# Two-layer hybrid trunk on one core: split weight parts kept in DRAM for a layer's second half, and a planner that counts DMA and PSUM banks

## The reference

```python
h = rmsnorm(x, pre_norm)
proj = jnp.einsum('bld,de->ble', h, w_in)          # 1024 -> 26 x 256 columns and 24 small ones
o_a = rmsnorm(gated_deltanet(silu(conv(gq, gk, gv)), gb, ga), gdn_norm) * silu(gz)      # 4 heads of 128
o_b = rmsnorm((ssd(silu(conv(sx, sB, sC)), sdt) + D * x) * silu(sz), ssd_norm)          # 16 heads of 64, 2 groups
o_c = rmsnorm(retention(rotary(rq), rotary(rk), rv), ret_norm) * silu(rg)               # 4 heads of 128
out = jnp.einsum('ble,ed->bld', concatenate([o_a, o_b, o_c]), w_out)
x = x + rmsnorm(out, post_norm)
```

## Time and profile before

| | before |
|---|---|
| median of 3 runs | 2435.17 us (2432.48 to 2436.13) |
| the profiled execution | 2434.56 us, its span 2432.8 us |
| TensorE busy | 2317.5 us, 95% |
| VectorE / ScalarE / GpSimd busy | 1385.3 / 884.9 / 913.6 us |
| mean granted TensorE clock | 0.993 |
| moved by DMA | 175.68 MB |

### The profile page before, as it was taken

One profiled execution on the slowest core, in us unless ns is written; L12 is line 12 of the kernel. 1 busy time (PEld: TensorE's weight loads), 2 busy tenths in 40 slices (PEclk: granted clock), 3 DMA queues, 4 the chain that ended last, 5 costly groups with the idle time before them and its releaser, 6 DMA issues.

```text
span 2432.8 us, 37233 instructions
## 1 busy us (share of the span) xinstructions
PE 2317.5 (95%) x15032; PEld 2060.2 (85%) x15032; DVE 1385.3 (57%) x2268; ACT 884.9 (36%) x1599; POOL 913.6 (38%) x752
## 2 busy tenths in 40 slices
PE   5999989999999999999999999999999999999995
PEld 4787878999887888899888788889988878889995
DVE  3766577435666658734566656763455664773333
ACT  3644334223534434323353434412343442442200
POOL 2554433233544343333254433323334443342310
PEclk9999999999999999999999999999999999999998
DMA  3211111223211112322221111322321111131212
GB/s 129 76 53 52 53 35 45 78 87 104 70 61 44 61 45 96 104 70 88 103 70 61 44 53 47 119 87 74 106 81 61 60 45 53 61 113 62 87 53 96
DMA packets 33722, 175.68 MB, mean 72 GB/s; under 512 B 3984, under 2 KB 4752, under 8 KB 20112
## 3 DMA queue, kind: packets, MB, share of 16 engines
q1 hardware_dynamic: 32832, 171.85, 20.8%
q10 hardware_dynamic: 720, 1.45, 0.2%
HBM read 164.90 MB, written 8.39 MB: 71 GB/s over the span
## 4 chain that ended last, share of the span: by engine, by line
PE 72%; DVE 5%; issue 3%; DMA 1%; ACT 0%; POOL 0%; SPq 0%; DVEq 0%; ACTq 0%; POOLq 0%
PE ps L955 68%; PE ps L958 5%; DVE wk L1410 1%; DMA xfin<-x_mid 1%; DMA w_loaded<-in_w_in 0%; DVE wk L1387 0%; DVE gss L1363 0%; DVE slot L1316 0%; DVE gss L1372 0%; ACT junk L1709 0%; DVE acc L1503 0%; DVE wk L1390 0%; DVE wk L1394 0%; DVE wk L1402 0%; DVE acc L1589 0%
## 5 line engine op out<-in xcount | busy, mean ns | idle before, releaser
L1896 POOL TENSOR_TENSOR w_low<-w_loaded,w_hi 128x512 fp32r<-128x512 f32 x416 | 569.9, 1386 | 719.8 <-ACT w_hi L1644 719.6
L955 PE MATMUL ps<-w_hi,hT_hi 128*128 128x256 f32 x1792 | 530.8, 296 | 1.2 <-POOL w_low L1896 1.2
L955 PE MATMUL ps<-w_low,hT_hi 128*128 128x256 f32 x1792 | 505.7, 282 | 0.0
L955 PE MATMUL ps<-w_hi,hT_lo 128*128 128x256 f32 x1792 | 500.6, 279 | 0.0
L955 PE MATMUL ps<-wo_loaded,mixT 128*128 128x256 f32 x2048 | 459.6, 380 | 12.7 <-DVE wk L1376 12.1
L955 PEld LDWEIGHTS ps<-wo_loaded,mixT 128*128 128x128 f32 x2048 | 383.5, 190 | 68.7 <-DVE wk L1376 14.0
L955 PEld LDWEIGHTS ps<-wk 128*128 128x128 f32 x2336 | 297.2, 191 | 84.3 <-issue 29.7
L955 PE MATMUL ps<-wk 128*128 128x128 f32 (+2 forms) x2336 | 343.6, 286 | 18.6 <-DVE mixT L1489 4.0
L955 PEld LDWEIGHTS ps<-w_low,hT_hi 128*128 128x128 f32 x1792 | 340.9, 190 | 1.2 <-issue 0.2
L955 PEld LDWEIGHTS ps<-w_hi,hT_hi 128*128 128x128 f32 x1792 | 337.8, 189 | 3.6 <-POOL w_low L1896 2.0
L955 PEld LDWEIGHTS ps<-w_hi,hT_lo 128*128 128x128 f32 x1792 | 339.8, 190 | 0.0
(11 more groups left out here) (179 smaller groups left out, 2825.7 us busy)
## 6 DMA issues: line engine op xcount, KB each, us to landing
w_loaded<-in_w_in SPq DMA_DIRECT2D x104, 1024.0 KB, 4.9
wo_loaded<-in_w_out SPq DMA_DIRECT2D x64, 512.0 KB, 3.6
wk<-in_x SPq DMA_DIRECT2D x8, 512.0 KB, 4.2
xfin<-in_x SPq DMA_DIRECT2D x8, 512.0 KB, 5.4
x_mid<-acc SPq DMA_DIRECT2D x8, 512.0 KB, 2.9
wk<-x_mid SPq DMA_DIRECT2D x8, 512.0 KB, 3.6
xfin<-x_mid SPq DMA_DIRECT2D x8, 512.0 KB, 4.3
out<-acc SPq DMA_DIRECT2D x8, 512.0 KB, 2.9
```

The lines of the kernel that those rows point to most:

```text
L955: return nc.tensor.matmul(o, a, b, start=start, stop=stop)
L1896: tt(w_lo[at], wr[at], w_hi[at], ALU.subtract)\
```

## The change

- **Kept parts.** A DRAM scratch `w_split` holds the high and low parts of all 26 pieces. In parts 0 and 2, once a piece's first half is projected, SP stores both parts (entry `keep`, 2 transfers of 1 MB), and the next load of that ring slot waits for them (`w_kept`). In parts 1 and 3 SP loads the two parts instead of the raw piece, and no `split` steps stand in the plan for these pieces. Every load of a piece is now cut in two by columns, with a semaphore for each half (`w_in_sem[slot][j]`): two transfers of 0.5 MB in parts 0 and 2, four in parts 1 and 3. TensorE waits for `w_lo_ready` four times in a piece as before in parts 0 and 2, and for the load twice in parts 1 and 3.
- **The planner counts DMA.** It has a DMA clock: 3200 ns for 1 MB, 1700 more until a transfer has landed, for the loads and kept stores of input pieces (`load_piece`, `MB`).
- **The planner counts banks.** `bank_due` gives the time when the banks that a step needs are emptied; it enters `due` and TensorE's own clock. `emptied_by_act` says which engine empties a bank.
- **Choices.** `NEAR` goes from 150 to 300, `OUT_WAIT` from 1500 to 1000, `LATE` from 99999 to 0, so a slice that isn't due gives way to a step or `out` unit. An `out` unit is only taken if it is itself due within `NEAR`, and a missing `split` no longer counts as stuck.

The core of the diff:

```diff
@@ front_steps
-                    if 0 <= j < 4 and not odd and (p, i) != (PARTS - 1, len(PIECES) - 1):
+                    if 0 <= j < 4 and not odd and (p + (i == len(PIECES) - 1)) % 2 == 0 and (p, i) != (PARTS - 1, len(PIECES) - 1):
@@ make_plan
+    def dma(work, *after):
+        return run("dma", work, *after) + 1700
+    def load_piece(n, after=()):
+        for half in range(2):
+            at["w_in", n, half] = dma(MB if n // len(PIECES) % 2 else MB // 2, *after)
...
-            out = [("w_lo", n, kk // 2)] if half == 0 else []
+            out = [("w_in", n, kk // 4) if p % 2 else ("w_lo", n, kk // 2)] if half == 0 else []
...
-        pe = lambda w: run("pe", w, *after)
+        pe = lambda w: run("pe", w, *after, "banks")
...
-                mark(("w_in", n + W_RING), end + 5000)
+                load_piece(n + W_RING, ("n", ))
+            elif p % 2 == 0:
+                dma(2 * MB, ("w_lo", n, 3))
...
+    def bank_due(step):
+        tags = [tag for pool, tag in bank_uses(step) if pool == "mix"]
+        times = []
+        for j, tag in enumerate(tags):
+            n = len(held) + j - len(MIX_BANKS)
+            if 0 <= n < len(held):
+                times.append(at.get(("emptied", held[n]), FAR) - 440 * j)
+        return max(times, default=0)
...
+        for pool, tag in bank_uses(step):
+            if pool == "mix":
+                held.append(tag)
+                if (step[0], tag[-1]) != ("gdn_turn", "v"):
+                    at["emptied", tag] = clock["act" if emptied_by_act(step, tag) else "dve"] + 60
+        if step[0] == "gdn_x0":
+            at["emptied", ("gdn_turn", *step[1:], "v")] = clock["dve"] + 60
...
-        return max([at.get(e, 0) for e in needs(step)], default=0)
+        return max([at.get(e, 0) for e in needs(step)] + [bank_due(step)])
...
-        if outs and ("small", smalls) in done and (late or stuck or wait > OUT_WAIT and apart >= APART):
+        unit = outs[0] if outs and ("small", smalls) in done else None
+        if unit and due(unit) <= now + NEAR and (late or stuck or wait > OUT_WAIT and apart >= APART):
...
-        elif not front_needs:
+        elif not front_needs and (not late or not (step or unit)):
...
-OUT_WAIT = 1500
-LATE = 99999
-NEAR = 150
+OUT_WAIT = 1000
+LATE = 0
+NEAR = 300
@@ sync
                     if n >= W_RING:
                         wait_filled(sp, ("proj", *divmod(n - W_RING, len(PIECES)), 1))
-                    sp.dma_start(wr[:, n % W_RING, :], w_in[p // 2, key[2]]).then_inc(w_in_sem[n % W_RING], 16)
+                        sp.wait_ge(w_kept[n % W_RING], kept_done(n - W_RING))
+                    for j in range(2):
+                        cols = slice(j * KD * PC // 2, (j + 1) * KD * PC // 2)
+                        if p % 2 == 0:
+                            sp.dma_start(wr[:, n % W_RING, cols], w_in[p // 2, key[2]][:, cols]).then_inc(w_in_sem[n % W_RING][j], 16)
+                        else:
+                            sp.dma_start(w_hi[:, n % W_RING, cols].bitcast(F32), w_split[key[2], 0][:, cols]).then_inc(w_in_sem[n % W_RING][j], 16)
+                            sp.dma_start(w_lo[:, n % W_RING, cols].bitcast(F32), w_split[key[2], 1][:, cols]).then_inc(w_in_sem[n % W_RING][j], 16)
+                elif kind == "keep":
+                    sp.wait_ge(S["w_lo_ready"], 4 * split_no(n) + 4)
+                    sp.dma_start(w_split[key[2], 0], w_hi[:, n % W_RING, :].bitcast(F32)).then_inc(w_kept[n % W_RING], 16)
+                    sp.dma_start(w_split[key[2], 1], w_lo[:, n % W_RING, :].bitcast(F32)).then_inc(w_kept[n % W_RING], 16)
@@ tensor, proj
-                            pe.wait_ge(S["w_lo_ready"], 4 * n + kk // 2 + 1)
+                            if p % 2 == 0:
+                                pe.wait_ge(S["w_lo_ready"], 4 * split_no(n) + kk // 2 + 1)
+                            elif kk % 4 == 0:
+                                pe.wait_ge(w_in_sem[n % W_RING][kk // 4], loads_done(n))
```

More of the change, by code:

```diff
@@ L489, in play @@
             mark(("xf", p, r[0] + 1), clock["dve"] + 5500)
+    for n in range(W_RING):
+        load_piece(n)
     done, smalls = {("small", -1)}, -1
@@ L493, in make_plan @@
     turns = [("mix_turn", p, g) for p in range(PARTS) for g in range(GROUPS)]
+    held = []
+    def bank_due(step):
[6 more added lines that the diff above has]
+        return max(times, default=0)
     def emit(step):
         plan.append(step)
+        at["banks"] = bank_due(step)
         play(step)
         done.add(step)
+        for pool, tag in bank_uses(step):
[5 more added lines that the diff above has]
+            at["emptied", ("gdn_turn", *step[1:], "v")] = clock["dve"] + 60
         if step[0] == "split_small":
@@ L552, in make_plan @@
         late = not front_needs and due(front[front_at][0]) > now + LATE
-        stuck = any(n and n[0] != "rescale" for n in front_needs) or front_at == len(front)
-        if outs and ("small", smalls) in done and (late or stuck or wait > OUT_WAIT and apart >= APART):
+        stuck = any(n and n[0] not in ("split", "rescale") for n in front_needs) or front_at == len(front)
+        unit = outs[0] if outs and ("small", smalls) in done else None
+        if unit and due(unit) <= now + NEAR and (late or stuck or wait > OUT_WAIT and apart >= APART):
             emit(outs.pop(0))
             apart = 0
-        elif not front_needs:
+        elif not front_needs and (not late or not (step or unit)):
             apart += front[front_at][0][0] == "proj"
@@ L560, in make_plan @@
             front_at += 1
-        elif front_needs[0] and front_needs[0][0] in ("split", "rescale"):
+        elif front_needs and front_needs[0] and front_needs[0][0] in ("split", "rescale"):
             chain = sides["split" if front_needs[0][0] == "split" else "scale"]
@@ L564, in make_plan, with emptied_by_act, split_no, loads_done @@
         else:
-            later = [x for x in (step, side, *turns[:1]) if x and known(x)]
+            later = [x for x in (step, side, unit, *turns[:1], *([] if front_needs else [front[front_at][0]])) if x and known(x)]
+            later = [due(x) for x in later if due(x) < FAR]
             assert later, (mix[mix_at:mix_at + 1], front[front_at:front_at + 1], front_needs)
-            clock["pe"] = max(now + 1, min(due(x) for x in later))
+            clock["pe"] = max(now + 1, min(later))
     return plan
+def emptied_by_act(step, tag):
+    k = step[0]
+    return (k in ("small", "small2", "gdn_x0", "x_turn") or k == "gdn_p" and tag == step
+            or (k, tag[-1]) in (("gdn_turn", "q"), ("gdn_s", "q"), ("bc_turn", 0), ("ret_turn", "k")))
 def half_after(p, i, half):
     return ("proj", p, i + half, 1 - half, Q - 1)
-OUT_WAIT = 1500
-LATE = 99999
+OUT_WAIT = 1000
+LATE = 0
 SPLIT_FROM = 6
 APART = 20
-NEAR = 150
-SLICE, LINE, TURN, UNIT, TABLE = 705, 224, 109, 16 * 216, 1283
+NEAR = 300
+FAR = 1e12
+SLICE, LINE, TURN, UNIT, TABLE, MB = 705, 224, 109, 16 * 216, 1283, 3200
+def split_no(n):
+    return n - len(PIECES) * ((n // len(PIECES) + 1) // 2)
+def loads_done(n):
+    return sum(32 if m // len(PIECES) % 2 else 16 for m in range(n % W_RING, n + 1, W_RING))
+def kept_done(n):
+    return sum(32 for m in range(n % W_RING, n + 1, W_RING) if m // len(PIECES) % 2 == 0)
 def slot_of(p, i, half):
@@ L681, in hybrid_kernel @@
     x1 = nc.dram_tensor("x_mid", (SEQ, D), F32, kind="Internal").ap()
+    w_split = nc.dram_tensor("w_split", (len(PIECES), 2, P, KD * PC), F32, kind="Internal").ap()
     with ExitStack() as ctx:
@@ L761, in hybrid_kernel @@
         loaded = sem("consts_loaded")
-        w_in_sem = [sem(f"piece_loaded{i}") for i in range(W_RING)]
+        w_in_sem = [[sem(f"piece_loaded{i}_{j}") for j in range(2)] for i in range(W_RING)]
+        w_kept = [sem(f"piece_kept{i}") for i in range(W_RING)]
         wo_in = [sem(f"unit_loaded{i}") for i in range(2)]
@@ L842, in hybrid_kernel @@
             loads.append((where[release] if n >= W_RING else -2, n, ("in", p, i)))
+            if p % 2 == 0:
+                loads.append((where["proj", p, i, 0, Q - 1], n, ("keep", p, i)))
         for n in range(PARTS * NT):
```

13 lines of the change are left out of this document (8 added, 5 removed).

## The result

| | before | after |
|---|---|---|
| median, us | 2435.44 (5 runs, 2432.48 to 2439.86) | 2444.73 (5 runs, 2443.67 to 2446.74) |
| ratio after / before | | 1.0038, 95% interval 1.0023 to 1.0052 |
| the profiled execution, its span | 2434.56, 2432.8 | 2446.74, 2444.9 |
| TensorE busy | 2317.5 us | 2334.6 us |
| mean granted TensorE clock | 0.993 | 0.992 |

The change makes the kernel 9.3 us slower, 0.38%. The forecast was 2438, and the result lies in the likeliest case's own range of 2425 to 2452; slower had the largest chance, 0.43. The margin between gain and loss was small, and this result lies on the side of the second rival: more direct pairs than forecast, though without its clock falls. The two profiled executions lie 12.1 us apart in span, 2.8 more than the medians, so what is read from the two traces adds up to more than 9.3.

A forecast was written before the change was run, and what follows sets the result against it. TensorE, busy 95% of the span, was taken to bound the kernel. Terms -24 (banks), -1 (low parts), +22 (direct pairs), +4, +2 and 0 gave +3 us: 2435.2 to 2438, likeliest 2425 to 2452, wide 2408 to 2470.

The forecast's parts named there:

- the likeliest case: Whole kernel: bank savings and direct-pair costs nearly cancel, 2438 us, own range 2425 to 2452; chance 0.40.
- the second rival: DeltaNet stages: all pairs become direct, costing 36 us instead of 22, and the clock falls, 14 us: 2466; chance 0.22.
- Part 1, splits: ScalarE and GpSimd splits dropped in the second halves: TensorE does not wait there, 0 us, between 0 and -2.
- Part 2, transfers: Kept stores and larger loads on the SP queue: covered by projection time, 0 us, bounds -1 and +8.
- Part 3, banks: TensorE's waits for full PSUM banks in parts 1 to 3: 24 us of 28.4 saved, bounds 0 and 30.
- Part 4, direct pairs: DeltaNet `gdn_s`/`gdn_v` and `gdn_o`/`gdn_s` without a slice between: 53 pairs at 0.41 us, +22 us, bounds 0 and 45.
- Other steps early: Some 16 other steps come a little early under NEAR 300, 0.25 us each: +4 us, bounds 0 and 12.
- Single `out` units: `out` units put singly between slices by OUT_WAIT and LATE: 20 more changes of 0.09 us, +2 us (0 to 6).
- that the pairs don't come: DeltaNet chunks: VectorE is busier in the model, so banks pay and pairs seldom become direct: 2414 us; chance 0.27.
- the slower one: The second rival, all pairs direct and clock falls: 2466 us, deciding from about 60 direct pairs without any fall; chance 0.22.
- That the transfers bind: Pieces that stand back to back: 0.3 us late for each of some 26, 8 us, 2446; chance 0.05.
- That the plan hardly changes: Planner: modelled bank emptying is too early, so bank waits stay and NEAR acts little: 2435 us; chance 0.06.

The follow-up runs named there:

- e1: Kernel before with the change's DRAM scratch, stores and half loads, its old order of steps, without splits in parts 1 and 3: 2433.74 us, ratio 0.9984.
- e8: Changed kernel without kept parts, every piece loaded raw and split in every part, planner as changed: 2447.16 us, ratio 1.0042.
- e9: Changed kernel with NEAR 150, OUT_WAIT 1500 and LATE 99999 as before, bank and DMA counting and kept parts retained: 2451.78 us, ratio 1.0064.
- e6: Changed kernel with the modelled `resid` and `state` VectorE times 310 instead of 300 ns in parts 1 and 3 alone: 2429.86 us, ratio 0.997.
- e5: Changed kernel with the modelled VectorE copies of `ret_turn` at 1350 instead of 1250 ns: 2439.73 us, ratio 1.0013.
- e10: Changed kernel with `resid` and `state` 310 ns in parts 1 and 3, `ret_turn` 1350, `ret_o` state work 350 instead of 250: 2421.39 us, ratio 0.9941.
- e2: Changed kernel with NEAR alone set back from 300 to 150: 2433.98 us, ratio 0.9986.
- e4: Changed kernel with the modelled state update of `gdn_o` at 310 instead of 300 ns in all parts: 2447.5 us, ratio 1.0041.

## Why the prediction was right, and where its steps were off

The mechanism was right, banks against direct pairs with transfers and splits at nothing, and so was the likelier sign (0.43 against 0.38 for faster). The size of the sum, +3 us, was too small, and that it came so near is in part luck: the banks gave about 13 us more than said and what stood against them took about 24 more. By its steps:

- **Part 1, splits: 0 said, between 0 and -2.** e1 has -3.4 for splits and transfers together, e8 no gain that can be told from none. VectorE did get faster as GpSimd fell silent. Windows of part 1 (busy of PE, PEld, DVE, ACT, POOL, clock, DMA share, GB/s), against the earlier trace rows:

```profile
588.00:1180.00 592.00, 581.37 (x3771) 512.38 (x3769) 314.61 (x567) 168.53 (x290) 90.43 (x87) 1.00 0.35 115
1180.00:1772.00 592.00, 579.82 (x3746) 512.21 (x3745) 345.81 (x566) 217.14 (x404) 230.12 (x183) 1.00 0.48 169
```

  GpSimd falls from 228.1 to 90.4 us, VectorE from 345.2 to 314.6 with the same 567 instructions, and the part takes 3.5 us longer. The Trainium skill (SBUF — State Buffer, Who interferes with whom) says that a VectorE instruction with two SBUF inputs contends with a GpSimd instruction that reads SBUF. The trace agrees: 30.6 us of VectorE time vanish in the part without splits, and the mean of the convolution's operation falls from 1080 to 969 ns. The time shows none of it.

- **Part 2, transfers: 0, right by e1, with a step that was too small.** SP was said to be held 2 to 6 us by a piece's stores (and 0.5 MB in 3.6 us is 146 GB/s, not 142). The stores land after 7.7 and 9.7 us (median), above all rows, and SP's own row of waits is

```profile
SPq L981 <- DMA w_split<-w_low: 374.8, 47, 11.9
```

  that is 8.0 us each and 11.9 at the longest, a little over the upper bound of 11.6. The cover held: TensorE waits for no DMA, and its waits for low parts grow by 2.8 us only. The sum of that part stood on the spacing of the pieces, and not on the price of a store. The share of the queue, 39%, was right. The Trainium skill (DMA: Bandwidth & Descriptors, Bandwidth) asks for transfers of 1 MiB and more. The trace agrees in kind: a raw half of 0.5 MB lands in the 4.9 us that a whole piece took the earlier trace rows. In the time the cut cost nothing that e1 shows.

- **Part 3, banks: -24 said (-25 with the low parts), -38 found.** This is a term mis-sized. All of the 28.4 us of listed waits went, no rest stayed; from start to start they are 31.7 (13.7, 13.5 and 4.5). On top went the 6.7 us behind line 1468 in part 0, listed with 6.5, which the rows showed and the sum left in place. The waits for low parts, from which 1 us was to come, grew instead. In the parts where nothing else interferes e9 shows the net of it, -5.8 and -8.3 us, where the sum has 8 a part. The price of a change from a mixing product to a projection, 0.09 us, was misread. The second product of a slice does come 0.09 late, but the first comes early by nearly as much. In before, eight `wk` products followed by a wide slice:

```profile
654.74 1.05 PE L955 MATMUL ps<-wk 128*128 128x128 f32 x8
655.55 0.48 PE L955 MATMUL ps<-hT_hi,w_hi 128*128 128x512 f32 x1
655.87 0.40 PE L955 MATMUL ps<-hT_hi,w_low 128*128 128x512 f32 x1
```

  Such products follow each other after 0.11 us, so seven steps are 0.78, and the slice starts 0.03 us after the eighth product. Over the 233 such entries into a narrow slice in before the two steps together take 0.232 us (median), where 0.11 and 0.12 back to back are 0.229. A change costs next to nothing. The price of a direct pair stands, for it was counted from 698.25, which is already such an early start.

- **Part 4, direct pairs: +22 said, +27.5 found.** 67 new ones instead of 53: the share of 60% was too low. The two orders aren't alike: `gdn_s` to `gdn_v` is direct in 47 of the 48 places counted, so the other VectorE work that was to push it past the 4 ns of margin hardly stood there; `gdn_o` to `gdn_s` is direct in 27 of 48. The price of 0.41 was good: 0.41 on average by the ledger (0.43 for the first kind, 0.37 for the second), 0.47 by e6.

- **Other steps early: +4 said, about +10 found** in the two kinds that were traced, within 0 to 12. The ledger has 4.6 us more from slices to other `wk` steps; if those are of this kind too, which wasn't tested, it is 14, above the bound. `ret_s` (12 x 0.4 us; e5: -5.0 without it) and `ret_o` (4 x 1.1, 4.9 by the ledger; e10: at most about -2) both fall under NEAR = 300. I hadn't gone through the model's lines for the retention as I had for `gdn_s`: at 300 each mark whose lead is between 150 and 300 changes its step, and they can be listed from the planner's code alone.

- **Single `out` units: +2,** not tested by itself. It was 20 more changes at 0.09 us. The plan enters the projection from other work 491 times and not 537; 67 pairs alone would make it 470, so 21 more did come from elsewhere, but at the price just found they cost nothing that can be told.

The rivals: that the pairs don't come is refuted by the timeline. Of the slower one, half came true: it was to decide from 60 pairs without any fall of the clock, and there were 67. In the DeltaNet stages of parts 1 to 3 the clock never fell in after. The stretch that was slow in before is at full clock; of the slow ones that stand elsewhere, this one in part 0 lies behind a wait of 2.7 us for a low part:

```profile
216.00:220.00 4.00, 3.07 (x23) 2.66 (x23) 1.27 (x4) 0.96 (x3) 0.00 (x0) 1.00 0.96 362
...
239.00:244.00 5.00, 3.59 (x10) 2.90 (x11) 4.93 (x5) 3.22 (x5) 5.00 (x4) 0.66 0.32 131
```

By the clock records the half level holds 17 us before the last 25 in both kernels. That the transfers bind is refuted by e1. That the plan hardly changes is refuted by the bank waits, which are gone.

**What stays open.** Some +10 us of the ledger lie in many small gaps, and 4.6 between slices and `wk` steps; neither was traced to a cause. Why the ratio of e1 is under 1 at all wasn't settled. No run shows the gain of the banks by itself in parts 0 and 2; there it is read from the ledger alone.

## What to carry to other kernels

When a planner's threshold is widened, list from its model every step whose lead falls between the old value and the new, and price each with one timeline of the place: here four kinds of such steps (`gdn_v`, `gdn_s`, `ret_s`, `ret_o`) took back 37 of the 38 us that counting banks had won. Change one threshold for one stage at a time, for a filler that is put between two steps is missing at a later one (e2, e4, e9), and the stage that runs out of it may lose more than all the others gain. Read stalls between short products from start to start, since half of such a stall is listed as busy time, and read a change of kind over both starts around it.

## What the runs showed of the hardware

- The clock fell here with no long idle spell before it. In e9 the granted clock is 1.00 from 1521.4 us to 1528.0, TensorE is listed busy for 4.2 of these 6.6 us, and no idle spell listed there is over 0.83 us; from 1528.2 on it is 0.50 (1.2 GHz) for 17 us. In e2 it is 0.67 as a mean over 1512 to 1538, with 20.7 of 26 us busy. The Trainium skill (TensorE: Matmul & The Clock Gate, A second HAM failure mode: psum-queue depth-cycling) describes a clock that oscillates because of frequent short idles between groups of products. The trace agrees in kind, with spells of 0.72 to 0.83 us. After, with one or two slices in each chunk, stays at 1.00 in its DeltaNet stages of parts 1 to 3.
- A store of 1 MB from SBUF to DRAM beside its twin lands after 7.7 and 9.7 us, where a load of 1 MB took 4.9 and a store of 0.5 MB 2.9.
- 164 MB more of traffic, 140 GB/s as a mean instead of 72, left TensorE's busy time as it was (e1: 2317.3 us against 2317.5).
- The first product of a narrow projection slice starts 0.03 us after a plain fp32 product of 128 columns, and its second one 0.20 us later; back to back the steps are 0.11 and 0.12.
